# Paged scores kept as rows per page, attention heads mixed and scored in pairs with outputs channel-first, and output-projection products issued in the last attention steps

## The reference

```python
for l in range(DEPTH):                       # DEPTH = 2
    hn = rmsnorm(xp, norm_mix[l])            # 256 prompt tokens
    q_nope, q_rope, c_kv, k_r, qb, kb, vb, g = project_in(hn, ...)
    a_out = mla_prompt(...)                  # 6 heads, latent attention, causal, 64 channels a head
    b_out = combine_dilations([dilated_prompt(qb, kb, vb, w, d) for w, d in ((128,1),(512,4),(2048,16))])
    c_out = conv_module(...)                 # 256 channels, 31 taps
    xp = xp + concat([a_out, b_out, c_out]) @ w_out[l]      # 1024 x 1024
    xp = xp + peer_blocked(rmsnorm(xp), ...)
    # the same for 8 samples with one new token each, whose past is 16 pages of 128 tokens:
    past_c = cache_kv_latent[l][page_table]  # (8, 2048, 128)
    past_r = cache_k_rope[l][page_table]     # (8, 2048, 32)
    s_past = q_lat . past_c + q_rope . past_r               # 6 heads x 2048 keys for each sample
    p = softmax([s_past, s_new]);  o_lat = p . past_c;  o = o_lat . w_uv
```

## Time and profile before

| what | value |
|---|---|
| median of 3 runs | 2066.7 us (2066.27 to 2067.76) |
| time of the profiled execution | 2067.32 us, its span 2065.4 us |
| PE busy | 2043.7 us, 99% of the span |
| DVE busy | 1557.4 us, 75% |
| ACT busy | 1300.2 us, 63% |
| granted TensorE clock | 0.996 of full speed |
| attention loop of layer 0, from the first scores to "ol" of the last sample | about 90.2 to 180.0 us |
| attention loop of layer 1 | about 1115.2 to 1204.9 us |

### The profile page before, as it was taken

How to read it: one execution, slowest core, us unless ns; L and a number is a source line. 1 busy time by engine, 2 the same in 40 slices (tenths; PEclk the granted TensorE clock), 3 DMA queues, 4 the chain that set the end, 5 groups by cost and what they waited for, 6 DMA issues and landing times.

```text
span 2065.4 us, 40864 instructions
## 1 busy us (share of the span) xinstructions
PE 2043.7 (99%) x15610; PEld 1805.3 (87%) x15610; DVE 1557.4 (75%) x3543; ACT 1300.2 (63%) x2567; POOL 118.9 (6%) x138
## 2 busy tenths in 40 slices
PE   9999999999999999999999999999999999999998
PEld 7777899999999888788887769999999998887887
DVE  6855789868899776676677466999688997766766
ACT  5466445658888655565564564556688876655654
POOL 2200010000000010100022000000000001101000
PEclk9999999999999999999999999999999999999999
DMA  9453447776666898898763543677766668988886
GB/s 324 145 162 134 162 153 254 248 252 221 208 220 220 282 314 284 302 322 281 248 228 142 171 164 124 200 252 252 241 220 215 214 218 300 317 287 293 267 268 221
DMA packets 137377, 481.78 MB, mean 233 GB/s; under 512 B 25666, under 2 KB 42082, under 8 KB 130768
## 3 DMA queue, kind: packets, MB, share of 16 engines
q1 hardware_dynamic: 124640, 438.45, 63.6%
q0 software_dynamic: 10496, 40.42, 5.6%
q10 hardware_dynamic: 2048, 0.30, 0.1%
HBM read 475.83 MB, written 104.21 MB: 281 GB/s over the span
## 4 chain that ended last, share of the span: by engine, by line
PE 96%; DVE 2%; ACT 1%; DMA 1%; issue 0%; DVEq 0%; ACTq 0%
PE ps L1226 36%; PE ps L1273 33%; PE ps L842 4%; PE ps L930 3%; PE ps L1238 3%; PE ps L1189 2%; PE ps L938 2%; PE ps L1197 2%; PE ps L1193 1%; PE ps L886 1%; PE ps L1153 1%; PE ps L1027 1%; PE ps L1212 1%; PE ps L895 1%; PE ps L1030 1%; DMA big<-in_peer_wq 1%
## 5 line engine op out<-in xcount | busy, mean ns | idle before, releaser
L2220 DVE TENSOR_TENSOR parts<-region,parts 128x1024 fp32r<-128x1024 f32 x512 | 625.7, 1222 | 300.6 <-ACT parts L1548 298.3
L1226 PE MATMUL ps<-tokens_hi,parts 128*128 128x256 f32 x4096 | 760.5, 284 | 0.0
L1548 ACT CAST parts<-region 128x1024 fp32r<-128x1024 f32 x512 | 538.7, 1052 | 271.1 <-PE ps L1273 207.5
L1273 PE MATMUL ps<-parts,parts_hw 128*128 128x512 f32 x3024 | 688.7, 390 | 0.0
L1273 PEld LDWEIGHTS ps<-parts,parts_hw 128*128 128x128 f32 x3024 | 567.0, 188 | 123.8 <-DVE parts_hw L2270 6.9
L1226 PEld LDWEIGHTS ps<-tokens_hi,parts 128*128 128x128 f32 x4096 | 636.9, 188 | 1.0 <-issue 0.6
L1226 PE MATMUL ps<-parts_hw,parts 128*128 128x256 f32 x2048 | 574.1, 280 | 0.0
L1226 PEld LDWEIGHTS ps<-parts_hw,parts 128*128 128x128 f32 x2048 | 386.8, 189 | 0.0
L1594 ACT ACTIVATE big<-ps 128x256 f32<-128x256 f32 (+31 forms) x252 | 131.7, 522 | 146.9 <-PE ps L1226 146.9
L1582 ACT CAST parts_hw<-big 128x256 fp32r<-128x256 f32 x256 | 170.6, 666 | 0.7 <-DVE big L2281 0.7
L1575 ACT ACTIVATE region<-region 128x128 f16<-128x128 f16 x512 | 169.3, 436 | 0.0
(11 more groups left out here) (328 smaller groups left out, 2244.8 us busy)
## 6 DMA issues: line engine op xcount, KB each, us to landing
region<-in_peer_uT SPq DMA_DIRECT2D x256, 512.0 KB, 4.0
region<-in_peer_v SPq DMA_DIRECT2D x256, 512.0 KB, 4.8
out<-in_state_win_k SPq DMA_DIRECT2D x112, 384.0 KB, 4.8
out<-in_state_win_v SPq DMA_DIRECT2D x112, 384.0 KB, 5.0
big<-in_window_keysT SPq DMA_DIRECT2D x16, 576.0 KB, 5.5
big<-in_state_win_v SPq DMA_DIRECT2D x48, 192.0 KB, 4.5
region<-in_w_out SPq DMA_DIRECT2D x4, 2048.0 KB, 9.0
big<-in_peer_wq SPq DMA_DIRECT2D x4, 2048.0 KB, 11.1
```

The source lines that it names most:

```text
L1226: mm = pe.matmul(ps[:, j % ZB, 0:SEQ], a, hp[b][:, c, :], start=(c == 0 and n == 0), stop=(c == KD - 1 and n == 2))
L1273: mm = pe.matmul(ps[:, 2 * half + t, :], w_t[a][:, 128 * t:128 * t + 128], v_t[b][:, 512 * half:512 * half + 512], start=(j == 0 and n == ...
L1548: act.copy(hi_t[n % HIGHS], rows_t[n % ROWS]).then_inc(high[l], 1)
L2220: dve.tensor_tensor(lo_t[n % ROWS], rows_t[n % ROWS], hi_t[n % HIGHS], ALU.subtract).then_inc(low[l], 1)
```

## The change

**Scores of the samples.** The latent queries stand in a wider padded row (`QL_PITCH` 56, the six heads from column 24), and four shifted slices of 32 columns put page `i` of a group into rows `8i` to `8i+5` of the group. So "SC" becomes 128 rows (8 for each of 16 pages) by 128 columns: 16 products of 128 columns for the latent part and 4 for the rotary part. Its maximum, exponential, transposes ("PP", one in place of four) and copies shrink to 128 columns. `PPs` gets zeroed gaps, which POOL sets.

**Heads.** DVE divides the probabilities before they are transposed (`divide`), and PE's "PT" waits for that. Two heads are mixed together, channel-first, in steps 3, 5, ... 13, ahead of "PT"; ACT and DVE split the result straight from PSUM, and "mT" is gone. The dilated heads are scored two at a time, in steps 6, 8 and 10, from the upper and lower 64 rows. DVE still takes the second of the two in the step after.

**Output projection.** ACT casts the first half's weights in step 11, ahead of the window outputs; PE makes the products of the first five of eight blocks (`EARLY`) in steps 12 and 13. Banks from "PT" of head 11 on are given from six, two being kept for the projection.

```diff
@@ job_plan
-        if s < 2 * NH:
-            jobs.append((("S", s), "V"))
+        jobs += [(("S", u), "V") for u in scored_in(s)]      # s; from 6 on s and s+1, at even s
...
+        if s >= 3 and s % 2:
+            jobs.append((("O", (s - 3) // 2), "V"))
...
-        if s >= 2:
-            jobs.append((("O", s - 2), "V"))
...
-    jobs += [(("mT", g), "V") for g in range(2 * HP)]
@@ PE
+                def dilated_scores(g):
+                    o = [begin("S", NH + 2 * g + n) for n in range(2)]
+                    for i, c0 in ((0, 0), (1, 128)):
+                        K = 128 * (i + 1)
+                        for n in range(2):
+                            r = slice(64 * n, 64 * n + 64)
+                            mm = pe.matmul(o[n][:, c0:c0 + K], qbT[r, g, 128 * i:128 * i + 128], kbT[r, g, 0:K], start=True, stop=True)
...
                 def turn_probs(u):
-                    pe.wait_ge(exp_ready, u + 1)
+                    pe.wait_ge(prob_ready, u + 1)
...
+                def mix_values(g):
+                    wait_moved(pe, "PT", 2 * g + 1)
...
+                    for k, (q0, q1, p0) in enumerate(((0, 256, 0), (128, 256, 256))):
+                        for n in range(2):
...
+                            mm = pe.matmul(o[64 * n:64 * n + 64, q0:q1], v, probT[:, n, p0:p0 + q1 - q0], start=(k == 0), stop=(k == 1),
@@ score_past
+                    for i in range(4):
+                        rows = slice(QL_AT - ROWS_OF_PAGE * i, QL_AT - ROWS_OF_PAGE * i + 32)
+                        for g in range(4):
+                            pe.matmul(o[32 * g:32 * g + 32, 0:128], qlS[:, b, rows], cT[:, g, 128 * i:128 * i + 128], start=(i == 0), stop=False,
...
                     for g in range(4):
-                        pe.matmul(o[32 * g:32 * g + 32, :], qlS[:, b, :], cT[:, g, :], start=True, stop=False, skip_group_check=True)
-                    for i in range(4):
-                        for g in range(4):
-                            mm = pe.matmul(o[32 * g:32 * g + NH, 128 * i:128 * i + 128], qrB[:, b, i, :], rT[:, g, :],
...
+                        mm = pe.matmul(o[32 * g:32 * g + 32, 0:128], qrB[:, b, :, :].rearrange("p i h -> p (i h)"), rT[:, g, :], start=False, stop=True,
...
-                    turn("PP", b, parts=[(Pm[:, 128 * i:128 * i + 128], 128, 128, 128 * i) for i in range(4)])
+                    turn("PP", b, parts=[(Pm[:, 0:128], 128, 128, 0)])
@@ PE, steps 12 and 13
                     if s == WINDOW_MIX + 1:
+                        wait_moved(pe, "O", EARLY - 1)
+                        out_high(0, 0, 0, EARLY)
                         wait_moved(pe, "ow", 1)
...
                     if s == WINDOW_MIX + 2:
+                        out_high(0, 1, 0, EARLY)
                         pe.wait_ge(wsel_ready, 1)
...
-                for g in range(2 * HP):
-                    turn("mT", g, parts=[(oAB[:, t, 128 * g:128 * g + 128], 128, 128, 128 * t) for t in range(2)])
...
                 for t in range(2):
-                    out_high(0, t)
+                    out_high(0, t, EARLY, KD)
@@ ACT, step 11
                     if s == WINDOW_MIX:
+                        act.wait_ge(product[now[0]], NUM["S", 2 * NH - 1] + 1)
+                        out_weights_high(0)
                         for n, dst in enumerate((owS, owS2)):
@@ DVE
+                def divide(u):
+                    dve.wait_ge(exp_ready, u + 1)
+                    step(dve.reciprocal(rden[:, u, :], den[:, u, :]))
+                    settle()
+                    for i, c0 in ((0, 0), (1, 128)):
+                        pr_ = prob[:, u % 2, c0:c0 + 128 * (i + 1)]
+                        e = dve.tensor_scalar(pr_, pr_, rden[:, u, i:i + 1], None, ALU.mult)
+                    e.then_inc(prob_ready, 1)
...
+                def low_heads(g):
+                    o = read("O", g)
...
+                    dve.wait_ge(mix_high, g + 1)
...
                     if s == EXT_STEP:
                         new_scores()
+                    if 1 <= s <= 2 * NH:
+                        divide(s - 1)
                     some_taps(TAPS[s] if s < len(TAPS) else 0)
```

More of the change, by code:

```diff
@@ L65 @@
 PT_TILE, PR_TILE = 34, 36
+ROWS_OF_PAGE = 8
 PAST_STEP = (0, 1, 2, 3, 5, 6, 8, 9)
@@ L85, with scored_in @@
 CONV_STEP = (8, 9, 10, 11, 12)
+EARLY = 5
+def scored_in(s):
+    if s < NH:
+        return [s]
+    return [s, s + 1] if s < 2 * NH and s % 2 == 0 else []
 def job_plan():
@@ L1142, in _ @@
                     turn("ycT", c, parts=tokens(yt, 128 * c))
[L1144 removed]
                 wait_moved(pe, "os")
[L1146 to L1154 removed]
+                wait_moved(pe, "O", 2 * HP - 1)
                 def out_low(c, t):
@@ L1445, in _, with out_weights_high, high_heads @@
                     act.copy(va[:, t, :], o[:, 0:384]).then_inc(moved_a[now[0]], 1)
+                def out_weights_high(c):
+                    act.wait_ge(w_ld[now[0]][(5 + c) % 2], 16 * ((5 + c) // 2))
+                    for k in range(KD):
+                        act.copy(out_high_part(c, k), wview(5 + c)[:, k, :]).then_inc(wo_high, 1)
+                def high_heads(g):
+                    o = arrive(act, "O", g)
+                    act.copy(mix_hi(g), o[:, 0:SEQ]).then_inc(mix_high, 1)
                 for s in range(2 * NH + 2):
@@ L1985, in _ @@
                         o = read("S", s)
+                        if s >= NH and s % 2:
+                            dve.wait_ge(product[now[0]], NUM["PT", s - 2] + 1)
                         for i, c0 in ((0, 0), (1, 128)):
@@ L1998, in _ @@
                         window_queries()
-                    u = s - 2
-                    if u >= 0:
-                        dve.wait_ge(exp_ready, u + 1)
-                        step(dve.reciprocal(rden[:, u, :], den[:, u, :]))
-                        o = read("O", u)
-                        settle()
-                        dve.tensor_tensor(oAB[:, :, 64 * u:64 * u + 64], o[:, 0:128].rearrange("p (t c) -> p t c", t=2),
-                                          rden[:, u, :].unsqueeze(2).to_broadcast([P, 2, 64]), ALU.mult).then_inc(moved_v[now[0]], 1)
+                    if s >= 3 and s % 2:
+                        low_heads((s - 3) // 2)
                     if s in WINDOW_STEP:
@@ L2024, in _ @@
                         conv_norm()
-                for g in range(2 * HP):
-                    o = read("mT", g)
-                    dve.wait_ge(mix_high, g + 1)
-                    dve.tensor_tensor(mix_lo[:, g, 0:SEQ], o[:, 0:SEQ], hiT[:, g, 0:SEQ], ALU.subtract).then_inc(moved_v[now[0]], 1)
                 o = read("os")
```

180 lines of the change are left out of this document (99 added, 81 removed).

## The result

The changed kernel takes **2083.9 us** (median of 4 runs, 2083.41 to 2087.07) against 2067.0 before: ratio 1.0085, 95% interval 1.007 to 1.010, so 0.85% slower and clear of the scatter. 2068.7 was forecast. The profiled execution took 2087.07 us (span 2085.3) and is the slowest of the four. Of its 19.8 us more than before, 18.9 lie between the first scores of a layer and the first transposes for PEER behind its projection, 9.1 and 9.8 in the two layers.

The account below looks back on a forecast made before the run. PE was taken to bound the loop; ycT, then DVE, then the last products the tail. Loop +0.3 and tail +0.8 us, times two layers, gave +2.2, taken as 2.0: median 2068.7 us, forecast 2062 to 2073, range 2059.5 to 2075.

Parts of the forecast that it names:

- the loop's sum: Attention loop, per layer: 15.4 us of new waits less 14.1 of PE work cut and 1.0 of idle time, +0.3 us.
- rival B: Low clock (1.2 GHz) moves ycT in the tail: +1.5 us in layer 0, +4 if layer 1 falls too; 2074.2 us, chance 0.12.
- D: Rival: pairs of products do not overlap on PE, 2 x 5.3 us more, 2079.3 us; chance 0.07.
- step 3: Loop: scores wait 0.5 us for a bank held by the first cT copy; "PP" and "ol" wait 0.9 for cT-copy banks.
- step 4: Loop, no past transposes: PE waits 1.9 us, as `low_heads(0)` on DVE waits for ACT, then new scores and division follow.
- step 6: Loop: "ol" waits 1.35 us for the bank of head 7's scores, which DVE takes only after its "SC" maximum.
- step 7: Loop: the pair's mix waits 1.1 us for `probT` of head 5.
- step 8: Loop: "ol" waits 2.1 us for the bank of head 9's scores, which DVE reaches late.
- step 10: Loop, step 9 to 10: the score pair waits 1.65 us for `low_heads(3)`, then "PT" of head 9 waits 1.5.
- step 11: Loop: "PT" of head 10 waits 3.5 us for its division, which stands behind the statistics on DVE.
- Tail: Behind the last "ol": early products delay ycT, conv output and DVE's low weights; 38.1 us for 37.3, +0.8 a layer.
- A: Rival: the early products pay, the tail 3.7 us a layer shorter in place of +0.8; 2059.9 us, chance 0.22.

Follow-up runs that it names:

- run 1: The changed kernel with 49 dummy products a layer put in front of eight waits of PE, nothing else: 2072.7 us.
- run 12: The whole changed kernel with the two DVE blocks (samples' convolution, statistics) one step later and dummies cut to the waits then left: 2065.4 us.
- run 11: The kernel before with the samples' part alone, DVE repeating part of the mask 8 times for heads 3, 7, 9 and 10 to add waits: 2060.4 us.
- run 2: The kernel before with only the change's part on the scores of the samples: 2051.5 us.
- run 3: The changed kernel with the dilated heads scored one by one in each step again: 2079.5 us.
- run 8: The kernel before with the samples' part and the dilated heads scored in pairs, mixes still one by one: 2051.4 us.
- run 6: The changed kernel with the division of one head's probabilities put ahead of the next head's mask and maximum on DVE: 2079.9 us.
- run 4: The changed kernel with two DVE blocks, the samples' convolution and the statistics, moved one step later behind the next division: 2071.4 us.

## Why the prediction was wrong

**The step that failed** is the loop's sum, "+0.3 us, that is no gain", by what it left to rival B: I held the low clock to be a matter of the tails, "each such stretch moves ycT by up to 4 us", because in the trace of before it fell once, at 188, with PE "busy throughout". I priced 15.4 us of waits a layer at their length and let PE's rows stand at 2.4 GHz between them. That gave a loop of 89.7 us. Measured, without the 2.6 of early products, it is 97.4 and 97.5: 15.5 us too long in the two layers, which is the whole miss of 15.2. What stands in its place is the low clock in the loops, most of it at or just behind the waits: 20.5 and 17.0 us, none before. Dummies in the waits give 11.2 us back (run 1), and together with DVE's order 18.5 (run 12); waits put into a kernel without them bring it (run 11).

**The rest of the 15.2 us miss** is 4.0 (run 1 against 2068.7). It lies in run 1's loops, which are together 4.7 us above the forecast. Waits plus dummies of run 1 are 16.3 us in each, 1.7 more than twice the 15.4 (and 3.1 more than the waits without dummies, the dummies' overhang). The stretch at 110.9 costs 1.8, the difference between the two loops. And PE's cut was a little too large: in layer 1 of run 1, at a clock of 1.00 throughout, the loop is 93.74 less 5.83 idle, 10.4 dummies and 2.6 early products, 74.9 of work for 88.4, a cut of 13.5 where I had 14.1.

**Point by point.** *Samples' part*: 7.9 us a layer summed; run 2's loops are 7.2 shorter at the same clock, with 0.2 more idle, so 7.4, and the rest of its 15.5 us lies in the tails. "SC" is 1.24 us as forecast. Right, 0.5 too large. *Pairs of scores*: the 2.4 is in PE's rows, but waits take most of it (runs 3 and 8). D was wrong. *Waits*: step 3 0.5 + 0.9 against 0.50 + 0.85 + 0.19; step 4 1.9, 1.83; step 6 1.35, 1.30; step 7 1.1, 0.98; step 8 2.1, 2.33; step 9 0.75, 0.85; step 10 1.65 + 1.5, 1.58 + 1.39; step 11 3.5, 2.46 and 3.29. Right each but the last in layer 0, 1.0 too long. *Tail*: the order of its chain was right (the wait at block 6, "3 us or more", is 2.67 and 2.84, ended by DVE). Its +0.8 a layer is best read in run 12, where the low clock of the tails falls almost on dummies alone: 37.05 + 2.6 and 37.04 + 2.6 us for 40.31 and 38.28. That is +1.4 in layer 1, from which the sum was made, and -0.7 in layer 0, where the kernel before has its 10.2 us of low clock. (The terms that lead to 32.0 there add to 31.7.) A was wrong: the early products cost 5.6 us. *B*: right in name, wrong in place and price; it had 2074.2, from low clock in both tails and none in the loops.

**What stays open.** Why run 6 has less low clock than the changed kernel with as much idle time, no run shows. Nor does any show why the clock falls behind one wait and not behind another of the same length, or why it falls at 87 and 110.9 in some executions, without a wait before it.

## What to carry to other kernels

When a change trades PE work for waits in a dense stretch, price the products behind the waits at both clock levels, not only the waits: here removed waits gave back between their own length (run 3) and about twice that (run 4), and added ones cost one and a half times theirs (run 11). Read the granted clock by windows for each stretch before trusting the chain, which books slowed products as PE work, and the mean clock of every execution beside its time, since one profiled execution can be the best or the worst of its kernel. And try the parts of a composite change alone: one part held all of the gain, and what was built around it (pairs, a division ahead of the transposes, early products) made the kernel 32 us slower than that part alone.

## What the runs showed of the hardware

Two products in opposite row halves (64 rows each) run side by side: 0.85 us to the next row for a pair (run 8) and for one head. PE's granted clock fell to 1.2 GHz beside idle notes of 1.4 to 3.3 us in the changed kernel's loops and behind one of 2.01 in run 11, and stayed at 2.4 GHz where dummy products took the place of most of that idle time (1.00 in the window 168.90 to 182.50, 0.50 without). It also fell where PE had not idled (at 110.9 in run 8). The row of 16 latent products of "SC" (L1072) takes 1.08 us at the one level and up to 1.94 at the other, the 20 transposes 2.40 and 4.07. Within one kernel the time goes with the mean granted clock, some 1.4 us for a thousandth.
